# Constant matmuls in five of TensorE's waits of a two-layer decoder kernel

## What is computed

```
h = rms_norm(x, ln_mix_g);  x = x + mixer(h)      # gated conv, 8-head latent attention, conformer conv
h = rms_norm(x, ln_ffn_g);  x = x + hier_moe(h)   # 32 experts, 2 of them for each token
h = rms_norm(x, ln_ple_g);  x = x + sigmoid(h @ w_ple_gate) * (p @ w_ple)
```

## Time and profile before

| | us |
|---|---|
| median of 3 runs | 1221.47 |
| the three runs | 1214.88, 1221.47, 1222.12 |
| the profiled execution: its own time | 1220.91 |
| its span, first to last instruction | 1219.1 |
| TensorE matmuls busy in the span | 1109.5 (91%) |
| mean granted TensorE clock | 0.963 |

### The profile page before, as it was taken

One profiled execution on the slowest core, in us unless ns is written; L12 is line 12 of the kernel. 1 busy time (PEld: TensorE's weight loads), 2 busy tenths in 40 slices (PEclk: granted clock), 3 DMA queues, 4 the chain that ended last, 5 costly groups with the idle time before them and its releaser, 6 DMA issues.

```text
span 1219.1 us, 21751 instructions
## 1 busy us (share of the span) xinstructions
PE 1109.5 (91%) x8140; PEld 872.4 (72%) x8140; DVE 647.8 (53%) x1351; ACT 356.3 (29%) x591; POOL 138.3 (11%) x169
## 2 busy tenths in 40 slices
PE   5988989999889999997879879999997999999975
PEld 4977979998645555554879779899985555555555
DVE  5784877555533333333668659775446233333355
ACT  4344443233321111112444344423334111111132
POOL 0111220011000010100102022101101010101001
PEclk9998999999989999999889989999998999999987
DMA  6634976546259999997435369664554799999941
GB/s 175 172 99 123 345 219 189 155 139 191 104 203 406 417 416 418 417 418 277 131 95 152 112 209 315 183 180 115 170 149 172 308 416 417 418 417 417 413 117 69
DMA packets 202707, 300.53 MB, mean 247 GB/s; under 512 B 13969, under 2 KB 166513, under 8 KB 186225
## 3 DMA queue, kind: packets, MB, share of 16 engines
q1 hardware_dynamic: 202608, 299.28, 69.4%
HBM read 298.21 MB, written 1.05 MB: 245 GB/s over the span
## 4 chain that ended last, share of the span: by engine, by line
PE 74%; DVE 10%; DMA 8%; issue 3%; ACT 3%; SPq 1%; POOL 0%; ACTq 0%; DVEq 0%; POOLq 0%
PE ps L695 72%; DMA gu_ring<-in_w_exp_up_dram 4%; DMA ring<-in_w_in_dram 3%; PE ps L698 2%; DVE wsplit L1606 2%; ACT wsplit L1140 1%; DMA ring<-in_w_uq_dram 1%; DVE work L1712 1%; DVE work L1632 1%; SPq L558 1%; DVE work L1684 1%; SPq L562 0%; DVE work L1569 0%; DVE h_pair L1615 0%; ACT lent_down L1140 0%
## 5 line engine op out<-in xcount | busy, mean ns | idle before, releaser
L695 PE MATMUL ps<-h_pair,wsplit 128*128 128x256 f32 x3264 | 427.7, 292 | 39.8 <-DVE h_pair L1615 12.2
L695 PEld LDWEIGHTS ps<-h_pair,wsplit 128*128 128x128 f32 x3264 | 413.1, 198 | 50.9 <-issue 34.1
L1606 DVE TENSOR_TENSOR wsplit<-ring,wsplit 128x1024 fp32r<-128x1024 f32 x136 | 167.7, 1236 | 98.7 <-ACT wsplit L1140 95.6
L1140 ACT ACTIVATE wsplit<-ring 128x1024 fp32r<-128x1024 f32 x136 | 142.0, 1056 | 220.1 <-PE ps L695 143.8
L695 PE MATMUL ps<-gu_ring,hT 128*64 128x256 f32 x1280 | 159.8, 391 | 9.9 <-issue 7.6
L695 PEld LDWEIGHTS ps<-gu_ring,hT 128*64 128x64 f32 x1280 | 90.6, 140 | 77.1 <-issue 32.9
L1342 ACT ACTIVATE prow<-ps 128x128 f32<-128x128 f32 x64 | 17.8, 278 | 291.3 <-PE ps L695 291.3
L1712 DVE SCALAR_TENSOR_TENSOR work<-work,convT 128x256 f32<-128x256 f32 x240 | 100.9, 494 | 0.0
L1961 DVE TENSOR_TENSOR prow<-prow,ps 128x128 f32<-128x128 f32 x64 | 18.5, 288 | 146.7 <-ACT prow L1342 146.7
L1975 DVE TENSOR_TENSOR hT_r<-ps,hT_r 128x512 fp32r<-128x512 f32 x64 | 44.3, 692 | 94.0 <-ACT hT_r L1140 94.0
L695 PE MATMUL ps<-work,ring 128*128 128x256 f32 x384 | 87.2, 383 | 0.0
(11 more groups left out here) (205 smaller groups left out, 1015.0 us busy)
## 6 DMA issues: line engine op xcount, KB each, us to landing
ring<-in_w_in_dram SPq DMA_DIRECT2D x104, 512.0 KB, 4.7
gu_ring<-in_w_exp_gate_dram SPq DMA_DIRECT2D x40, 1024.0 KB, 14.8
gu_ring<-in_w_exp_up_dram SPq DMA_DIRECT2D x40, 1024.0 KB, 16.9
down_ring<-in_w_exp_down_dram SPq DMA_DIRECT2D x40, 1024.0 KB, 19.0
lent_down<-in_w_exp_down_dram SPq DMA_DIRECT2D x24, 1024.0 KB, 19.5
ring<-in_w_exp_gate_dram SPq DMA_DIRECT2D x12, 1024.0 KB, 14.7
ring<-in_w_exp_up_dram SPq DMA_DIRECT2D x12, 1024.0 KB, 16.9
lent_gate_up<-in_w_exp_gate_dram SPq DMA_DIRECT2D x12, 1024.0 KB, 15.6
```

What stands on the lines that cost most here:

```text
L695: return nc.tensor.matmul(o, lhsT, rhs, start=first, stop=last)
L1140: return nc.scalar.activation(o, i, ACT.Copy)
L1606: TT(tile_split[:, m, 1, :, :], tile_of(name, m), tile_split[:, m, 0, :, :].bitcast(F32), ALU.subtract).then_inc(tile_low, 1)
```

## The change

A helper `keep_busy(at, n)` issues n float32 matmuls of 128x128 by 128x512 on the constants `iota` into bank `at`. Nobody reads what they write, and every real product that uses the bank later starts by overwriting it. It is called at five places of each layer: three matmuls into bank 5 behind the two transposes at the layer's start; one into the bank of pp2 ahead of the gather, once pp2 is evacuated; one into bank 1 behind the gather, ahead of the value load and the branch; four into bank 3 behind the experts, ahead of pg0; and three into bank 3 at the end of the layer, ahead of the matmul that counts `engines_done`. That is twelve matmuls a layer. No other engine's program differs.

```diff
+            def keep_busy(at, n):
+
+                for _ in range(n):
+                    mm(ps[:, at, :], iota[:, 0:P], iota, True, True)
+
...
                 tr(ps[:, 6, 0:CROWS], crow[:, :], CROWS).then_inc(vec_tr, 1)
                 tr(ps[:, 7, 0:VROWS], vrow[:, :], VROWS).then_inc(vec_tr, 1)
+                keep_busy(5, 3)
                 project_split("kv", "mix")
...
                 embed(3)
 
+                wait_evacuated(pe, "pp2")
+                keep_busy(UI["pp2"] % BANKS, 1)
                 pe.wait_ge(tok_low, 4)
...
                 wait_evacuated(pe, "rank")
                 for m in range(1, 4):
                     wait_evacuated(pe, f"pp{m}")
+                keep_busy(1, 1)
                 pe.wait_ge(xs_pad, 3)
...
+                keep_busy(3, 4)
                 project_split("pg0", "ple")
...
                 pe.wait_ge(bcast_used, len(NORMS))
+                keep_busy(3, 3)
                 mm(ps[:, 3, 0:1], ones[:, :], ones[:, 0:1], True, True).then_inc(engines_done, 1)
```

## The result

The changed kernel takes 1201.3 us in the median of four runs (1200.75 to 1205.17), the kernel before 1221.1. The ratio is 0.9858, 95% interval 0.9824 to 0.9891: 1.4% faster. I had forecast 1217.5 us and a range that ends at 1211.5. The profiled execution took 1205.17 us, 15.7 less than that of before. The kernel's later second measurement gave 0.9867 (0.9838 to 0.9896).

What follows compares the result with a forecast made beforehand. TensorE, with matmuls filling 91% of the span, was taken as the bound over most of the kernel. Terms -1.8 - 1.0 - 0 - 1.3 - 0 = -4.1 us from 1220.91 gave 1216.8, adjusted to the runs' median and rounded to 1217.5; range 1211.5 to 1223.

Steps and rivals of the forecast that it cites:

- the fill ahead of the branch: Behind the gather: one fill, no cost, no gain; bounds 0.9 us a layer lost, 2.1 us a layer won.
- The clock part: Gains from a higher clock at the five fill places, summed to -4.1 us against the profiled 1220.91 us.
- Layer start: Three fills before kv: warm matmuls bring the statistics forward, 1.8 us gained over both layers; at worst 2.2 lost.
- the wait for the low tile: In kv after its first 16 matmuls: the next eight need VectorE's tile, ready at 620.1, hiding nearly all fill overrun.
- Ahead of the gather: One fill in the wait for `sel`: warmer gather matmuls, 1.0 us gained; ends 0.4 lost to 3.2 gained.
- the value load would wait for the fill: Before the branch: load delayed from 338.1 to 341.8, each layer 3.7 us later, 1224.2 us; chance 0.12.
- Behind the experts: Four fills before pg0: its last 36 matmuls partly warmer, 1.3 us gained for both layers; ends 2.6 gained, 1.0 lost.
- the clock falls all the same: Rival: fills end before the waits do and thin work follows two, so nothing moves, 1220 to 1222 us; chance 0.22.
- Layer end: Three fills before TensorE's count: cost nothing, VectorE's count still last; they only help the next layer-start fills.
- a gain ahead of expert 0 survives the experts: At the experts: they run at the weight stream's pace, and an earlier first expert starts that stream earlier.
- All cold time near the fills goes: Rival: 46% of 37 us cold matmul time near the fills is saved, 17 us, giving 1204 us; chance 0.05.
- a shift that I don't see: Remainder of the chances, for an unforeseen effect with no place or size given; chance 0.03.

Runs made afterwards that it cites:

- e2: Kernel before plus five unexecuted constant matmuls in the branch not taken, no fill, experts' code moved by 20 instructions: 1211.5 us, 0.9905 of before.
- e10: Second measurement of the kernel before plus five unexecuted constant matmuls, no fill: 1209.8 us, 0.9920 of before.
- e1: Changed kernel, all twelve fills, plus 59 unexecuted constant matmuls so the experts' code moves by 256 instructions: 1219.8 us, 0.9980 of the kernel before.
- e9: The changed kernel with all twelve fills, measured once more: 1204.7 us, 0.9867 of the kernel before.
- e12: Kernel before with TensorE's branch turned round and the five front fills, without the seven rear ones: 1198.4 us, 0.9826 of before.
- e11: Kernel before with TensorE's branch turned round, common experts' code directly behind it, no fill: 1203.8 us, 0.9863 of before.
- e4: Changed kernel without the seven fills behind the experts' code, keeping the five in front: 1204.6 us, 0.9846 of the kernel before.
- e3: Kernel before plus two unexecuted constant matmuls, no fill, experts' code moved by 8 instructions: 1223.6 us, 1.0001 of before.
- e7: Changed kernel with only the three layer-start fills, two unexecuted matmuls keeping the experts' code place: 1205.2 us, 0.9880 of the kernel before.
- e6: Changed kernel with only the fill ahead of the gather, four unexecuted matmuls keeping the experts' code place: 1208.0 us, 0.9896 of the kernel before.

## Why the prediction was wrong

**The step that failed** is the one on the fill ahead of the branch: "Nor do I give it a gain: the 3.39 us without a matmul from about 345.3 on are untouched". They were not. I had read the earlier trace rows as a fixed cost and the row's "issue" as if it were nothing, and then counted the instructions that the change adds as time alone. They are also a place: 20 instructions ahead of the experts' code moved the end of a code piece from inside expert 0 to just ahead of it. e2 and e10 put that by itself at 10 to 11 us, 5.4 us a layer. The term stood at 0, and even its bound of 2.1 us a layer held only the cold half of the stretch.

**The clock part was right in size, in part by luck.** All other terms and this fill's share of the clock came to -4.1 us. The fills measured -2.6 (e1 against before, not told from nothing), -5.1 (e9 against e10) and, with the branch turned round, -5.4 (e12 against e11), the last with front fills only. But of the single terms below only those for the start and the end of a layer came out; the others were off and made up for each other. The gains seen in the stretches come to some 3 us, so the rest of the 5 is not placed.

*Layer start:* forecast -1.8 for both layers. The table gives -0.8 in layer 0 and -0.9 in layer 1 on the means, with 0.14 us lost in layer 1 of the changed kernel because kv starts later. The steps held. This is the timeline of the changed kernel at the start of layer 1, against the earlier trace rows:

```profile
604.77 4.54 PE L695 MATMUL ps<-cst 128*128 128x512 f32 x6
609.09 2.45 PE L695 MATMUL ps<-h_pair,wsplit 128*128 128x256 f32 x16
611.94 4.10 PE L695 MATMUL ps<-h_pair,wsplit 128*128 128x256 f32 x32 [0.40 <-DVE wsplit L1617]
```

The fills took 4.3 us, part of it cold, not the 5.1 of an all-cold run. The 16 matmuls ran warm, then came the wait for the low tile that I had named, and then 32 matmuls. The statistics follow 6.8 us behind the first matmul, where I had written 6.7.

*Ahead of the gather:* forecast -1.0. The means differ by 0.2 us a layer, with single values from 10.8 to 12.8: nothing that can be told. e1, with the fill, still ran a part of both gathers cold (mean clock 0.78 from 329 to 334 us and 0.61 from 922 to 926).

*Ahead of the branch:* forecast 0 for the clock. In the old place it is 0: expert 0 takes 10.9 and 10.75 us in e1. In the new place expert 0 is warm in all eight stretches with that fill and in five of eight without, 0.6 us a layer on the mean. That is too few to show that the fill does it: e10, without any, is warm in both layers. If it does, the move of the code opened the way, as no stall stands behind it any more. The rival that the value load would wait for the fill did not come: the load ran at 335.4 and the branch at 336.3, both ahead of the last gather matmuls and the fill at 338.0.

*Behind the experts:* forecast -1.3, measured nothing, 11.0 against 10.7 us. The rival "the clock falls all the same" was right here, and this is the view that shows it, windows of TensorE in the changed kernel (stretch, length, busy, granted clock, DMA share, GB/s):

```profile
569.40:574.30 4.90, 2.17 (x12) 1.00 0.68 204
574.35:580.20 5.85, 5.85 (x36) 0.71 0.10 28
605.00:609.00 4.00, 4.00 (x6) 0.57 0.02 6
```

The clock was up through the thin stretch, where it is worth nothing, and it fell within the 36 matmuls. The Trainium skill, TensorE: Matmul & The Clock Gate, HAM oscillation — how this bites in real kernels, prices a cold stretch by its duration; in these rows it counts as much on which work the stretch lies.

*Layer end:* forecast 0, and it is 0. VectorE's count stays last. From pg0's statistics to the next layer's first transpose it is 24.1 us in every kernel, with the fills or without.

**What carried.** I had said that a gain ahead of expert 0 survives the experts, as the weight stream starts only with the first slot used. It does: from the clearing matmuls to the last combine it is 219.6 to 220.7 us in before, after and e1 to e4 alike, both layers, and the stream still fills the DMA engines (answering to the earlier trace rows):

```profile
355.00:560.00 205.00, 202.11 (x1709) 1.00 1.02 411
```

**The rivals.** "All cold time near the fills goes", 1204 us, came within 3 us of the time with a chance of 0.05, and its mechanism is false: the start of layer 1 and pg0 still have cold stretches (0.57 and 0.71 above; the gathers of that execution ran warm), and e1 has all fills and no such gain. A right number here would have taught the wrong thing. The remainder of 0.03 "for a shift that I don't see" is where the truth was.

**What stays open.** Whether a move by 12 or 16 instructions would do was not tried. The mixer's length varies: from kv's statistics to the embedding it is 292.6 us in before, 288.3 in e1 and 295.6 in e3, layer 0, with cold stretches at changing places. The code there is the same in before and e3, and 12 instructions off in e1. It varies between executions of one kernel, too: e2 and e10 are the same kernel and have 292.6 and 295.2 us. No run isolates what varies, and it is why effects below some 3 us were read from the traces' own stretches. That the second code transfer comes so late behind the experts' branch was not isolated, either. Behind the jump back at the end of layer 0, with the DMA engines nearly idle (share 0.05), it starts 3.2 us after the first (607.04 and 610.26 in before), here, with the weights streaming, 6.2 us; that suggests that it queues behind the weights, and no run tests it.

## What to carry to other kernels

Adding or removing instructions on an engine moves all code behind them, and that can cost or gain more than the instructions themselves; put as many unexecuted ones in a branch not taken, and see, before crediting the change. A wait called "issue" in straight code at the same record in each pass is a candidate for that. Look whether a transfer of the code queue ends just before the engine resumes; their number alone fell with the stall here (54 to 52) but not in e11. Put the common side of a rare branch directly behind it. A fill that raises the clock pays only if dense work which nothing else holds back follows at once.

## What the runs showed of the hardware

A compare-and-branch on TensorE took 3.3 to 4.0 us to far code, over all runs, and 0.08 to 0.10 us where it goes on to the code right behind it, with no code transfer beside it. That difference is not one of jumping or not: the experts' inner loop jumps back twice a layer, in 0.21 to 0.26 us each, and in before no code transfer runs from 431 to 587 us, which takes in nearly all of its two later passes. The Trainium skill, Advanced Engine Details and Errata, Control Flow Timing, gives some 108 ns for one; the branch that goes straight on is near that, the jump back takes twice that, the far one over thirty times that, and the measurement decides. When the code ran out soon after such a jump, with the DMA engines full of weights, TensorE stood for 3.4 to 4.9 us.

The clock can be up at the start of layer 0 with nothing but transposes ahead. In e1 the first clock record, at full, is at 13.79 us, and the first fill starts at 14.08; e7 shows the same. In e6 and e11, without fills there, it rose at 14.6 and 13.2 us and was down again before kv had started, and these two have the longest kv of layer 0 (8.3 and 8.0 us). In the other kernels without these fills the first record is at 21.6 to 22.9 us. With the fills the clock was up by 16.3 us in all seven kernels and stayed up past 110 us, which is what they do for layer 0. This is the changed kernel, whose record rises at 14.87: from the first of the six records to the next it is 0.85 us, between the others 0.43. Without fills the cold rate of the earlier trace rows is read from 18.5 us on.

```profile
14.19 3.16 PE L695 MATMUL ps<-cst 128*128 128x512 f32 x6
```
